# Expert matmuls whose stationary operands lie 64, 128 or 192 bytes modulo 256 from their weights instead of at the same residue

## What is computed

```python
def swiglu(h, w1, w3, w2):
    return (jax.nn.silu(h @ w1) * (h @ w3)) @ w2

def moe_swiglu(h, router, w1, w3, w2):
    logits = (h @ router).astype(jnp.float32)
    top_v, top_i = lax.top_k(logits, TOP_K)          # TOP_K = 2
    gates = jax.nn.softmax(top_v, axis=-1)
    ...                                              # the tokens of each expert, in blocks of 128
    yb = lax.map(expert_block, (xb, block_e))        # swiglu(xb, w1[e], w3[e], w2[e])
    y = jnp.zeros((T + 1, D), h.dtype).at[row_tok].add(yb.reshape(n_rows, D) * row_w[:, None])
```

## Time and profile before

| what | value |
|---|---|
| median of 2 runs | 2029.37 us |
| the profiled execution's own time | 2030.57 us |
| its span | 2028.5 us |
| TensorE busy | 1980.4 us, 98% |
| VectorE busy | 1702.0 us, 84% |
| ScalarE busy | 1257.4 us, 62% |
| DMA, mean over the span | 290 GB/s |

### The profile page before, as it was taken

How to read it: one execution, slowest core, us unless ns; L and a number is a source line. 1 busy time by engine, 2 the same in 40 slices (tenths; PEclk the granted TensorE clock), 3 DMA queues, 4 the chain that set the end, 5 groups by cost and what they waited for, 6 DMA issues and landing times.

```text
span 2028.5 us, 32745 instructions
## 1 busy us (share of the span) xinstructions
PE 1980.4 (98%) x13665; PEld 1771.3 (87%) x13665; DVE 1702.0 (84%) x1874; ACT 1257.4 (62%) x1269; POOL 39.5 (2%) x77
## 2 busy tenths in 40 slices
PE   7999999999999999999999999999999999999997
PEld 6889999999879899999878888888888888888886
DVE  6797888998786778887479898898988989898997
ACT  3469735654344554343367777777777777777775
POOL 3010000000000000000000000000000000000000
PEclk8999999999999999999999999999999999999999
DMA  9974876878643459999259999999999999999994
GB/s 310 302 248 138 264 235 224 263 235 277 219 165 105 146 194 332 320 322 324 84 208 368 368 354 371 350 374 361 362 361 355 369 352 370 367 354 369 368 372 158
DMA packets 337577, 589.16 MB, mean 290 GB/s; under 512 B 10518, under 2 KB 150316, under 8 KB 337425
## 3 DMA queue, kind: packets, MB, share of 16 engines
q1 hardware_dynamic: 333776, 580.70, 81.6%
q0 software_dynamic: 3008, 5.78, 1.0%
q10 hardware_dynamic: 640, 0.52, 0.1%
HBM read 585.89 MB, written 1.07 MB: 289 GB/s over the span
## 4 chain that ended last, share of the span: by engine, by line
PE 86%; DVE 8%; issue 3%; ACT 2%; DMA 1%; SPq 0%; DVEq 0%; ACTq 0%
PE bk L669 15%; PE bk L671 15%; PE bk L670 15%; PE bk L663 10%; PE bk L664 10%; PE bk L665 10%; DVE wlo L1969 2%; DVE macc L1994 2%; PE bk L1214 1%; ACT whi L1351 1%; DMA raw<-in_w_mod 1%; DVE uc L2349 1%; PE bk L1263 1%; PE bk L1126 1%; PE bk L725 1%
## 5 line engine op out<-in xcount | busy, mean ns | idle before, releaser
L1969 DVE TENSOR_TENSOR wlo<-raw,whi 128x2048 fp32r<-128x2048 f32 x477 | 1080.3, 2267 | 204.5 <-ACT whi L1351 203.2
L1351 ACT CAST whi<-raw 128x2048 fp32r<-128x2048 f32 x477 | 903.7, 1895 | 376.6 <-PE bk L671 249.0
L663 PE MATMUL bk<-HH,whi 128*128 128x256 f32 x1480 | 420.6, 284 | 0.9 <-DVE KC L2245 0.4
L664 PE MATMUL bk<-HL,whi 128*128 128x256 f32 x1480 | 410.4, 277 | 0.0
L665 PE MATMUL bk<-HH,wlo 128*128 128x256 f32 x1480 | 409.0, 276 | 0.0
L669 PE MATMUL bk<-whi,xh 128*128 128x512 f32 x896 | 354.4, 396 | 0.0
L671 PE MATMUL bk<-wlo,xh 128*128 128x512 f32 x896 | 349.3, 390 | 0.0
L670 PE MATMUL bk<-whi,xl 128*128 128x512 f32 x896 | 349.0, 390 | 0.0
L663 PEld LDWEIGHTS bk<-HH,whi 128*128 128x128 f32 x1480 | 276.9, 187 | 6.6 <-issue 3.8
L664 PEld LDWEIGHTS bk<-HL,whi 128*128 128x128 f32 x1480 | 279.6, 189 | 1.1 <-issue 0.7
L665 PEld LDWEIGHTS bk<-HH,wlo 128*128 128x128 f32 x1480 | 276.9, 187 | 0.0
(11 more groups left out here) (378 smaller groups left out, 2465.2 us busy)
## 6 DMA issues: line engine op xcount, KB each, us to landing
raw<-in_moe_w SPq DMA_DIRECT2D x334, 1024.0 KB, 6.5
raw<-in_ada_w SPq DMA_DIRECT2D x56, 1024.0 KB, 5.6
raw<-in_ff_w SPq DMA_DIRECT2D x40, 1024.0 KB, 5.9
raw<-in_w_in SPq DMA_DIRECT2D x29, 1024.0 KB, 5.5
raw<-in_w_mod SPq DMA_DIRECT2D x24, 1024.0 KB, 5.7
raw<-in_w_up SPq DMA_DIRECT2D x22, 1024.0 KB, 5.1
raw<-in_attn_w_qkv SPq DMA_DIRECT2D x12, 1024.0 KB, 5.6
raw<-in_w_branch SPq DMA_DIRECT2D x8, 1024.0 KB, 5.2
```

Of the source, the lines that this page charges most:

```text
L663: pe.matmul(o, sh, mh, start=start, stop=False, skip_group_check=True)
L664: pe.matmul(o, sh, ml, start=False, stop=False, skip_group_check=True)
L1351: act.copy(halves_at(q, g)[0], raw[q.slot[i]][:, :n]).then_inc(q.hi_done.mark(g), 1)
L1969: dve.tensor_tensor(low, raw[q.slot[i]][:, :n], high.bitcast(F), ALU.subtract).then_inc(q.taken.mark(i), 1)
```

## The change

Only addresses change. Every engine runs the same instructions in the same order; the lines behind the removed table move up by three.

- `wlo` moves from residue 64 to 128 in all layers, and the 64 bytes that expert slabs were shifted by fall away: for them `wlo` stays at 128.
- The low token tiles of dense layers (HL, OL, HLc, HL2, FL, HL4, FL4, HL5) move from 192 to 0. The high ones stay at 192.
- The experts' stationary tiles move from 128 to: `xh0` 64, `xl0` 64, `xh1` 64, `xl1` 0, `tth0` 192, `ttl0` 192, `tth1` 0, `ttl1` 0.
- Without a wish of their own, `pb`, `ptt`, `YH` and `YL` go from 128 to 192, since they are laid behind those tiles. The token tiles `TH` and `TL` that the gather multiplies with `pb` stay at 224.

In the following table a distance is (address of the moving operand − address of the stationary operand of the next matmul) modulo 256, for the three matmuls of a chunk in their order.

| matmuls | before | after |
|---|---|---|
| dense, 256 columns (L663, L664, L665) | 64, 128, 64 | 64, 128, 64 |
| `natural`, 256 columns (L725, L726, L727) | 192, 192, 128 | 128, 192, 192 |
| experts w1, w3, pairs 0 and 2 | 0, 0, 0 | 64, 64, 64 |
| experts w1, w3, pairs 1 and 3 | 0, 0, 0 | 128, 64, 64 |
| experts w2, even steps | 0, 0, 0 | 192, 192, 192 |
| experts w2, odd steps | 0, 0, 0 | 128, 128, 128 |

```diff
@@ -223,7 +223,7 @@
         whi = [sb(f"whi{i}", [128, 2048], R, 128) for i in range(NP)]
-        wlo = [sb(f"wlo{i}", [128, 2064], R, 64) for i in range(NP)]
+        wlo = [sb(f"wlo{i}", [128, 2048], R, 128) for i in range(NP)]
@@ -238,7 +238,7 @@
-        HH, HL = sb("HH", [128, 8, S], R, 192), sb("HL", [128, 8, S], R, 192)
+        HH, HL = sb("HH", [128, 8, S], R, 192), sb("HL", [128, 8, S], R, 0)
...
@@ -313,12 +313,11 @@
-        XH = [sb(f"xh{i}", [128, 8, 256], R, 128) for i in range(2)]
-        XL = [sb(f"xl{i}", [128, 8, 256], R, 128) for i in range(2)]
+        XH, XL = zip(*((sb(f"xh{i}", [128, 8, 256], R, ph), sb(f"xl{i}", [128, 8, 256], R, pl)) for i, ph, pl in ((0, 64, 64), (1, 64, 0))))
+        TT, TTL = zip(*((sb(f"tth{i}", [128, 4, 128], R, ph), sb(f"ttl{i}", [128, 4, 128], R, pl)) for i, ph, pl in ((1, 0, 0), (0, 192, 192))))
+        TT, TTL = TT[::-1], TTL[::-1]
         PB = sb("pb", [128, 2, 256], R)
         PTT = [sb(f"ptt{i}", [128, 2, 256], R) for i in range(2)]
-        TT = [sb(f"tth{i}", [128, 4, 128], R, 128) for i in range(2)]
-        TTL = [sb(f"ttl{i}", [128, 4, 128], R, 128) for i in range(2)]
@@ -640,13 +639,11 @@
-        lies = {"w1": 16, "w3": 16, "w2": 16}
-
         def halves_at(q, g):
 
             i = q.gi[g]
-            e, n, k = lies.get(q.plan[i][1][0], 0), q.plan[i][3] * q.plan[i][4], g % NP
-            return whi[k][:, :n], wlo[k][:, e:e + n]
+            n, k = q.plan[i][3] * q.plan[i][4], g % NP
+            return whi[k][:, :n], wlo[k][:, :n]
```

More of the change, by code:

```diff
@@ L265, in build @@
         at[0] = mark
-        OH, OL = sb("OH", [128, 16, S], R, 192), sb("OL", [128, 16, S], R, 192)
+        OH, OL = sb("OH", [128, 16, S], R, 192), sb("OL", [128, 16, S], R, 0)
         at[0] = max(at[0], tail)
@@ L270, in build @@
         at[0] = base
-        HHc, HLc = sb("HHc", [128, 8, S], R, 192), sb("HLc", [128, 8, S], R, 192)
-        HH2, HL2 = sb("HH2", [128, 8, S], R, 192), sb("HL2", [128, 8, S], R, 192)
+        HHc, HLc = sb("HHc", [128, 8, S], R, 192), sb("HLc", [128, 8, S], R, 0)
+        HH2, HL2 = sb("HH2", [128, 8, S], R, 192), sb("HL2", [128, 8, S], R, 0)
         mark = at[0]
-        FH, FL = sb("FH", [128, 22, S], R, 192), sb("FL", [128, 22, S], R, 192)
+        FH, FL = sb("FH", [128, 22, S], R, 192), sb("FL", [128, 22, S], R, 0)
         UC = [sb(f"uc{i}", [128, 2, S]) for i in range(3)]
@@ L292, in build @@
         mark2 = at[0]
-        HH4, HL4 = sb("HH4", [128, 8, S], R, 192), sb("HL4", [128, 8, S], R, 192)
-        FH4, FL4 = sb("FH4", [128, 28, S], R, 192), sb("FL4", [128, 28, S], R, 192)
+        HH4, HL4 = sb("HH4", [128, 8, S], R, 192), sb("HL4", [128, 8, S], R, 0)
+        FH4, FL4 = sb("FH4", [128, 28, S], R, 192), sb("FL4", [128, 28, S], R, 0)
         UD = [sb(f"ud{i}", [128, 2, S]) for i in range(2)]
@@ L299, in build @@
         FN = sb("FN", [128, 2, 8, 256])
-        HH5, HL5 = sb("HH5", [128, 8, S], R, 192), sb("HL5", [128, 8, S], R, 192)
+        HH5, HL5 = sb("HH5", [128, 8, S], R, 192), sb("HL5", [128, 8, S], R, 0)
         at[0] = mark
```

## The result

The changed kernel takes 2055.86 us (median of 2 runs, 2054.66 to 2057.05) against 2029.37: 1.013 times the time of before, 95% interval 1.0087 to 1.0174, 26 us more. The forecast was 8 us less and its range ended at 2047; the sign was wrong.

A forecast was written before the change was run, and what follows sets the result against it. TensorE was taken as the bound. Terms summed to a gain of 7 to 16 us if the loss carries over, else 0; the middle, 8 us, off 2029.4 gave 2021 us, with an 8-in-10 range of 2005 to 2047.

The forecast's parts named there:

- What bounds the kernel: Whole kernel, expert stage above all: TensorE busy 98% of the span, so changed matmul steps enter the time almost one for one.
- Dense layers ... I cost it at 0.: Dense layers, L663 to L665: all distances stay, so 0; a change of pace would be 11 us, either sign.
- If the loss carries over from 256 columns as it stands.: Experts' w1 and w3: loss per matmul would be 6.5 to 9 ns in place of 10.7, as in 256-column layers.
- the estimate of 109: Estimated undisturbed price of a 256-column float32r matmul: 106.7 + 2.7 = 109 ns; for 512 columns 216 ns.
- The one row pair: Scatter, 256 columns, and experts, 512, both at distance 0: losses of 8 to 14 ns against 10.7, read as about the same.
- w1 and w3: Experts' w1 and w3, 2688 matmuls: a gain of 1.7 to 4.2 ns each, 5 to 11 us.
- w2: Experts' w2, 1344 matmuls: gain of 0.8 us for the half at distance 192, 1 to 3 us for that at 128.
- Rival 1: Experts' new distances never settle: 4.3 ns more on 4032 matmuls, +17 us, 2047; w2 alone +6 us; chance 0.3.
- Rival 3: Experts: most of the 10.7 ns loss per matmul goes, 2011 to 2002 us, or 1986 if all; chance 0.1.
- Natural, gather, scatter: Attention values: 0, bounds 3 ns either way; gather and scatter, 256 matmuls of 256 columns: under 1 us at 3 ns.
- Wrong at its root if the dense layers ... move by more than a few us.: The prediction's own test: dense layers, whose distances stay, should keep 115.5 ns and the branch layer 117.9.
- The rule on two read ports: TensorE's two independent SBUF read ports: weight loads take no read bandwidth, so addresses would not matter and time stays 2029.4 us.

The follow-up runs named there:

- the last versions: Kernel before with dense distances equal: 64 measured 2036.76 us, 128 and 192 by layer 2036.78 us, 192 in every dense product 2023.95 us, ratio 0.9955.

## Why the prediction was wrong, point by point

- **What bounds the kernel.** Right. TensorE's distance from start to start went into the time: 15.7 us in the expert stage from 16.6 us of longer steps, and neither VectorE nor the DMAs took a part. Outside the experts cover was not complete: 1,757 dense triples that went from 832 to 848 clocks are 11.7 us, and 8.1 arrived. VectorE's share of the chain fell from 8% to 6%, which fits stretches where it was the later one; this was not tested.
- **"Dense layers ... I cost it at 0."** This step failed. It rested on the distances staying 64, 128, 64. The run with only the dense tiles moved has those distances and about 117.8 ns in every layer, +0.28%. The prediction had the size at hand (2.4 ns on 3 x 1480 matmuls, 11 us; the stage lost 8.1) and had seen the second pace in the branch layer. Its sentence "I see no reason for either sign" was the error: the layer of the earlier trace rows was on the quicker of the two paces that the rows showed, and so, as a full reading shows, were 1,757 of the 1,977 undisturbed dense triples; the rest are the branch layer and short or not yet settled stretches. Between these two paces a change of state could only cost. The branch layer, already on the slower one, did not move.
- **"If the loss carries over from 256 columns as it stands."** This failed for the experts, in sign. It holds at distance 0: 120.0 ns for 256 columns is 11 over the estimate of 109, and 226.7 for 512 is 10.7 over 216. At 64, 64, 64 it does not: 256 columns at 113.3 or 117.8 ns lose 4 or 9, 512 columns at 229.0 lose 13. At equal distances 128 the losses are 9.7 and 16.6. The one row pair on which the step was built happened to be the one distance at which widths agree.
- **w1 and w3**: forecast a gain of 1.7 to 4.2 ns, measured a loss of 1.7 and 4.4. **w2**: forecast a gain of about 2 to 4 us, measured a loss of 6.6 and 5.9 ns on 672 matmuls each, 8.4 us. The third of the matmuls that the forecast thought least of carries half of the experts' loss.
- **Rival 1** had the size for the experts: +17 us with 4.3 ns a matmul; measured 15.7, or 3.9 ns on 4032. Its mechanism, a stream that never settles, is not what the trace shows. With `xh0` the steps settle: 229.0 ns is the third of 1648 clocks, and most triples have that length. With the others the steps vary from one to the next, between 226 and 241 ns, as rival 1 wants them, but after the first six steps nearly every stretch (24 matmuls) repeats a fixed cycle, read to the nanosecond: odd pairs one of six steps and 3328 clocks (45 of 56 stretches), even turns one of two steps and 1120 clocks (24 of 27), odd turns one of seven steps and 3904 clocks (19 of 27). They settled, on slower cycles. It got 0.3 where the forecast got 0.45, and its upper end, 2047, left out that the dense layers could move as well.
- **Rival 3** looked for a large gain in the 10.7 ns. No set of places that was tried took any of it from 512 columns. For 256 columns the last versions took some: 113.3 ns are 4 over the estimate of 109, where the earlier trace rows has 6.5.
- **Natural, gather, scatter** were costed at nothing or under 1 us. Natural went from 118.7 to 118.3 ns, 0.2 us less. In gather and scatter no form's mean step moved by more than 1.1 ns (`ptt` against `YH`, 118.5 to 119.6), under 0.3 us in all.
- **"Wrong at its root if the dense layers ... move by more than a few us."** They moved 8.1, and so it is.
- **The rule on two read ports** (the Trainium skill, "TensorE: Matmul & The Clock Gate", "Step-by-step: what each phase is for") was rightly doubted: with nothing but addresses changed, the time went from 2023.95 to 2065.0 us. Whether it is the reads of the two ports that meet, no run shows. Another page of the Trainium skill, "SBUF — State Buffer", section "Operand start alignment", states where an operand may start and says that this is "about legality, not speed"; the runs add that speed does depend on it, through the place of one operand against the other.

What stays open: what in the chip sets the lengths of a triple, and what makes a stretch fall on one or the other. In all traces a dense stretch settles within its first four triples and then keeps its pace up to the next interruption or the next tile, and the pace can differ at equal addresses (HH4 before and with only the experts' tiles moved). That the moment of the restart decides it is only argued.

## What to carry to other kernels

Where TensorE is the bound and streams matmul after matmul, the places of stationary and moving operands modulo 256 are worth some per cent of its time, and the best place has to be measured for each width: distance 0 was best for 512 columns and among the worst for 256, where 192 was best. Scan several sets in one kernel, one per layer, and read the step from start to start in the timeline, since busy times hide it. When a row shows two paces for one case, cost the change of state by which of the two the kernel is on now: on the quicker one it loses, unless there is a third that no row shows yet, as the 816 clocks here.

## What the runs showed of the hardware that was not expected

- Settled streams repeat a cycle whose length is a multiple of 16 clocks. Often the cycle is one triple, of 816, 832, 848 or 864 clocks for 256 columns and 1632, 1648, 1664 or 1680 for 512; it can be two steps (1120 clocks), six (3328), seven (3904) or five triples (4272). 16 clocks more are 6.7 ns a triple, 2.2 ns a matmul.
- One set of places can have two paces (816 and 848 at equal distances 64 and 192; 832 and 848 at 64, 128, 64), and a stretch, once settled, keeps its own until something comes between.
- Moving every operand by the same 64 bytes changes nothing (1.000, 0.9988 to 1.0011).
- With no instruction changed and only addresses moved, the kernels of this study lie between 2023.95 and 2065.0 us, 2% apart.
